# Output projection of the second block: part of its products moved between the chunks of the delta rule

## The reference, cut to what matters

```python
attn = rms_norm_2(neighbourhood_attention(aq, ak, hs(av), rpb), attn_out_g)
dn = bidirectional_gated_deltanet(dqkv, dz, dab[:, :, 0], dab[:, :, 1], ...)
x = x + jnp.concatenate([attn, dn], axis=-1) @ w_out
x = x + hierarchical_moe(rms_norm_2(x, ln2_g), ...)
```

```python
def step(state, inp):
    v_new = u_c - w_c @ state
    o_c = (q_c * exp(g_c)) @ state + qk_c @ v_new
    state = state * exp(g_last) + (k_c * exp(g_last - g_c)).T @ v_new
```

## Time and profile before

| what | value |
|---|---|
| runs | 2626.96, 2631.46, 2630.94 us; median 2630.94 us |
| the profiled execution's own time | 2627.38 us |
| its span | 2625.6 us |
| PE busy / PE weight loads busy | 2264.3 us (86%) / 1665.9 us (63%) |
| DVE / ACT / POOL busy | 1178.7 (45%) / 868.3 (33%) / 163.4 us (6%) |
| mean granted TensorE clock | 0.894 |
| moved | 377.26 MB, mean 144 GB/s |

### The profile page before, as it was taken

How to read it: one execution, slowest core, us unless ns; L and a number is a source line. 1 busy time by engine, 2 the same in 40 slices (tenths; PEclk the granted TensorE clock), 3 DMA queues, 4 the chain that set the end, 5 groups by cost and what they waited for, 6 DMA issues and landing times. The chain is left out here.

```text
span 2625.6 us, 32561 instructions
## 1 busy us (share of the span) xinstructions
PE 2264.3 (86%) x13812; PEld 1665.9 (63%) x13812; DVE 1178.7 (45%) x1868; ACT 868.3 (33%) x1294; POOL 163.4 (6%) x174
## 2 busy tenths in 40 slices
PE   8999999958997877899999899877988688888885
PEld 7787888847675775687888777656967333333332
DVE  4456664365583665575663435655343311111112
ACT  5344443255652223453442254543122110000000
POOL 0000000000001210000000000002200011111110
PEclk9899999978998777899999999967667799999998
DMA  5122222212111001222223223211014599999996
GB/s 198 65 92 85 94 99 78 99 64 100 61 65 18 14 15 49 89 83 94 96 82 100 92 89 119 79 20 17 2 49 181 239 419 416 417 409 405 403 402 253
DMA packets 106741, 377.26 MB, mean 144 GB/s; under 512 B 54976, under 2 KB 55760, under 8 KB 67680
## 3 DMA queue, kind: packets, MB, share of 16 engines
q1 hardware_dynamic: 84992, 296.44, 30.6%
q10 hardware_dynamic: 9216, 67.11, 6.2%
q0 software_dynamic: 12384, 11.58, 1.5%
HBM read 375.31 MB, written 27.53 MB: 153 GB/s over the span
## 5 line engine op out<-in xcount | busy, mean ns | idle before, releaser
L593 PE MATMUL ps<-xh,wh 128*128 128x512 f32 x1288 | 515.6, 400 | 68.5 <-DVE wl L557 45.2
L594 PE MATMUL ps<-xl,wh 128*128 128x512 f32 x1288 | 510.6, 396 | 0.0
L595 PE MATMUL ps<-xh,wl 128*128 128x512 f32 x1288 | 508.9, 395 | 0.0
L557 DVE TENSOR_TENSOR wl<-raw,wh 128x2048 fp32r<-128x2048 f32 (+2 forms) x127 | 264.3, 2081 | 285.5 <-ACT wh L551 285.5
L3462 PE MATMUL ps<-egu,XT 128*64 128x512 f32 x1088 | 273.5, 660 | 85.1 <-DMA egu<-e_up 81.3
L593 PEld LDWEIGHTS ps<-xh,wh 128*128 128x128 f32 x1288 | 247.1, 192 | 134.8 <-DVE wl L557 55.3
L595 PEld LDWEIGHTS ps<-xh,wl 128*128 128x128 f32 x1288 | 247.2, 192 | 53.7
L594 PEld LDWEIGHTS ps<-xl,wh 128*128 128x128 f32 x1288 | 247.9, 192 | 51.0 <-issue 0.2
L551 ACT ACTIVATE wh<-raw 128x2048 fp32r<-128x2048 f32 (+2 forms) x127 | 220.3, 1736 | 91.4 <-PE ps L1072 69.2
L3462 PEld LDWEIGHTS ps<-egu,XT 128*64 128x64 f32 x1088 | 94.2, 152 | 240.9 <-issue 229.4
L3480 DVE TENSOR_TENSOR HIDT<-ps,SIL 128x256 f32<-128x256 f32 x34 | 14.4, 425 | 352.0 <-ACT SIL L3472 352.0
(11 more groups left out here) (531 smaller groups left out, 3390.3 us busy)
## 6 DMA issues: line engine op xcount, KB each, us to landing
egu<-e_gate SPq DMA_DIRECT2D x68, 1024.0 KB, 14.3
egu<-e_up SPq DMA_DIRECT2D x68, 1024.0 KB, 25.3
ed<-e_down ACTq DMA_DIRECT2D x64, 1024.0 KB, 11.0
raw<-up SPq DMA_DIRECT2D x44, 1024.0 KB, 4.9
raw<-down SPq DMA_DIRECT2D x32, 704.0 KB, 4.2
raw<-rwkv_kr SPq DMA_DIRECT2D x8, 1024.0 KB, 4.9
raw<-in_dn SPq DMA_DIRECT2D x8, 1024.0 KB, 4.9
raw<-sgu_v SPq DMA_DIRECT2D x4, 1024.0 KB, 10.3
```

Of the source, the lines that this page charges most:

```text
L557: e.tensor_tensor(K.WL[s][:, 0:n], K.RAW[r][:, 0:n], K.WH[s][:, 0:n].bitcast(F32), SUB).then_inc(*K.w_low.mark(i))
L593: e.matmul(o, h[:, q, k], x_high[:, k], start=k == 0, stop=False)
L594: e.matmul(o, h[:, q, k], x_low[:, k], start=False, stop=False)
L595: last = e.matmul(o, l[:, q, k], x_high[:, k], start=False, stop=k == KT - 1)
```

## The change

- Tiles 0 to 3 of the input (the attention's features) and the first half (k = 0 to 3) of weight items 0 and 1 get buffers of their own, which overlay the attention's tiles and the old queries. SP loads these weights (2 x 512 KB) after the queries are scaled, ACT and DVE split them between the two pairs of the solve.
- PE makes four triples between w and the recurrence, then one after `s` and one after `o` in every step until twelve are done (three output tiles x four input tiles). So steps 0 to 3 have two each and steps 4 to 7 none.
- To free three PSUM banks, both directions of `ws` share bank 0, and the others move down by one.
- Item 2 and the second halves of items 0 and 1 are loaded from the end of w on, ACT splits item 2's high half after its last output copy.
- `out2_*` is written anew: fourth tile's early part, items 2 and 3, and k = 4 to 7 of the tiles begun. The squares go to a buffer of their own.
- PE's point "out2" is now taken behind the last triple.

Cut to its core (buffers, PSUM bank numbers and signals left out):

```diff
@@ delta_pe
         last.then_inc(*K.delta_sum.mark("w", x))
+    for q in range(1, 4):
+        for t in K.board.emptied(K.u["dn_w"] + q):
+            e.wait_ge(*t)
+    early = early_pe(K, e)
+    for _ in range(4):
+        next(early)
     K.board.point("PE", "solved")
...
             last.then_inc(*K.delta_sum.mark("s", s, d))
+        next(early, None)
...
         last.then_inc(*K.delta_sum.mark("o", s))
+        next(early, None)
+    for _ in early:
+        pass
@@ delta_act
         K.board.empty(u, K.act_delta("k", n))
+    for k in range(3):
+        e.activation(K.XHE[:, k], K.AT[:, k], ACT.Copy).then_inc(*K.x_high.mark("out2", k))
...
+        if pair == 0:
+            for i in range(2):
+                e.wait_ge(*K.early_in("raw", 1))
+                e.activation(K.WHE[:, i], K.RWE[:, i], ACT.Copy).then_inc(*K.w_high.mark("early", i))
+    e.activation(K.XHE3[:, :], K.AT[:, 3], ACT.Copy).then_inc(*K.x_high.mark("out2", 3))
...
+    third = K.first["out2"] + 2
+    e.wait_ge(*K.raw_in[0](third))
+    e.activation(K.WH[1][:, :], K.RAW[0][:, :], ACT.Copy).then_inc(*K.w_high.mark(third))
     K.board.point("ACT", "delta")
@@ delta_dve
+    for k in range(3):
+        x_low_dve(K, e, "out2", k, K.AT[:, k], K.XHE, K.XLE)
...
+        if pair == 0:
+            for i in range(2):
+                e.wait_ge(*K.w_high("early", i))
+                e.tensor_tensor(K.WLE[:, i], K.RWE[:, i], K.WHE[:, i].bitcast(F32), SUB).then_inc(*K.w_low.mark("early", i))
+    e.wait_ge(*K.x_high("out2", 3))
+    e.tensor_tensor(K.XLE[:, 3], K.AT[:, 3], K.XHE3[:, :].bitcast(F32), SUB).then_inc(*K.x_low.mark("out2", 3))
@@
+def early_pe(K, e, tiles=range(3)):
+
+    for i in range(2):
+        h, l = (x[:, i].rearrange("p (m k j) -> p m k j", m=2, k=4) for x in (K.WHE, K.WLE))
+        e.wait_ge(*K.w_low("early", i))
+        for k in range(4):
+            e.wait_ge(*K.x_low("out2", k))
+            for q in range(2):
+                if 2 * i + q in tiles:
+                    out2_triple(K, e, h[:, q, k], l[:, q, k], k, 2 * i + q)
+                    yield
@@ out2_sp
-    for t in K.board.all_at("delta"):
+    first, src = K.first["out2"], K.A["out2"]
+    for t in (K.delta_sum("k", 3), K.dve_delta("q", 1, 3)):
         e.wait_ge(*t)
-    load_weights(K, e, K.first["out2"], len(K.items))
+    for i in range(2):
+        e.dma_start(K.RWE[:, i].rearrange("p (m k) -> p m k", m=2), src[i].rearrange("p (m k) -> p m k", m=2)[:, :, 0:512]).then_inc(
+            *K.early_in.landing("raw", i))
+    e.wait_ge(*K.delta_sum("w", 3))
+    e.dma_start(K.RAW[0][:, :], src[2]).then_inc(*K.raw_in[0].landing(first + 2))
...
+    for i in range(2):
+        e.wait_ge(*K.w_low("half", i))
+    e.dma_start(K.RAW[1][:, :], src[3]).then_inc(*K.raw_in[1].landing(first + 3))
@@ out2_pe
+    for t in K.board.emptied(K.u["out2"] + 3 - 8):
+        e.wait_ge(*t)
+    for _ in early_pe(K, e, (3,)):
+        pass
+    whole(2, 1, range(4))
+    for i in range(2):
+        e.wait_ge(*K.w_low("half", i))
+        for k in range(4, KT):
+            e.wait_ge(*K.x_low("out2", k))
+            for q in range(2):
+                out2_triple(K, e, half_of(K.WH[0], i)[:, q, k - 4], half_of(K.WL[0], i)[:, q, k - 4], k, 2 * i + q)
+    whole(2, 1, range(4, KT))
+    whole(3, 0, range(KT))
     K.board.point("PE", "out2")
-    gemm_pe(K, e, "out2", "out2", KT, K.XH, K.XL)
@@ out2_act
-    for k in range(4):
-        e.activation(K.XH[:, k], K.AT[:, k], ACT.Copy).then_inc(*K.x_high.mark("out2", k))
-    weight_high(K, e, K.first["out2"])
+    half_high(K, e, 0)
...
+    half_high(K, e, 1)
     for h in range(4):
-        x_high_act(K, e, "out2", 4 + h, K.T[h], K.dve_delta("gated", h), K.XH)
+        x_high_act(K, e, "out2", 4 + h, K.SQO[:, h], K.dve_delta("gated", h), K.XH)
@@ out2_dve
-    for k in range(4):
-        x_low_dve(K, e, "out2", k, K.AT[:, k], K.XH, K.XL)
-    weight_low(K, e, K.first["out2"])
+    whole_low(2, 1)
+    half_low(K, e, 0)
...
         x_low_dve(K, e, "out2", 4 + h, x, K.XH, K.XL)
+        if h == 1:
+            half_low(K, e, 1)
```

More of the change, by code:

```diff
@@ L484, in uses @@
         at = 0
-        for name, n in (("sq_oo", 4), ("out2", 8), ("n_ln2", 1), ("route", 1), ("tok", 16), ("rank", 1), ("place", 1)):
+        for name, n in (("sq_oo", 5), ("out2", 8), ("n_ln2", 1), ("route", 1), ("tok", 16), ("rank", 1), ("place", 1)):
             self.u2[name] = 3000 + at
@@ L2902, in delta_pe @@
             for d, (ch, n, hf, p) in enumerate(geo):
-                last = e.matmul(K.ps[p, d, 128 * h:128 * h + 128], K.WT[:, hf, 16 * d + 4 * n + h], K.SS2[:, 0, 4 * d + h], start=True, stop=True)
+                last = e.matmul(K.ps[p, 0, 128 * h:128 * h + 128], K.WT[:, hf, 16 * d + 4 * n + h], K.SS2[:, 0, 4 * d + h], start=True, stop=True)
         last.then_inc(*K.delta_sum.mark("ws", s))
@@ L2915, in delta_pe @@
             for d, (ch, n, hf, p) in enumerate(geo):
-                last = e.matmul(K.ps[:, 2 + d, 128 * h:128 * h + 128], K.KD[p, 16 * d + 4 * n + h], K.VN[p, d, h], start=True, stop=True)
+                last = e.matmul(K.ps[:, 1 + d, 128 * h:128 * h + 128], K.KD[p, 16 * d + 4 * n + h], K.VN[p, d, h], start=True, stop=True)
         last.then_inc(*K.delta_sum.mark("kv", s))
@@ L3070, in delta_pool, with out2_rows, out2_triple @@
     K.board.point("POOL", "delta")
+def out2_rows(K, k):
+    if k < 4:
+        return K.XHE3[:, :] if k == 3 else K.XHE[:, k], K.XLE[:, k]
+    return K.XH[:, k], K.XL[:, k]
+def out2_triple(K, e, high, low, k, m):
+    o = K.ps[:, (K.u["out2"] + m) % 8]
+    xh, xl = out2_rows(K, k)
+    e.matmul(o, high, xh, start=k == 0, stop=False)
+    e.matmul(o, high, xl, start=False, stop=False)
+    last = e.matmul(o, low, xh, start=False, stop=k == KT - 1)
+    if k == KT - 1:
+        last.then_inc(*K.gemm_sum.mark("out2", m))
@@ L3082, in out2_pe, with half_low @@
+def half_low(K, e, i):
+    c = slice(1024 * i, 1024 * i + 1024)
+    e.wait_ge(*K.w_high("half", i))
+    e.tensor_tensor(K.WL[0][:, c], K.RAW[1][:, c], K.WH[0][:, c].bitcast(F32), SUB).then_inc(*K.w_low.mark("half", i))
 def out2_pe(K, e):
+    first = K.first["out2"]
     for t in K.board.all_at("delta"):
```

63 lines of the change are left out of this document (48 added, 15 removed).

## The result

| what | before | after |
|---|---|---|
| median of the runs made side by side (six each) | 2627.99 us | 2607.87 us |
| lowest and highest | 2621.87, 2631.46 us | 2604.31, 2611.99 us |
| the profiled execution: own time / span | 2627.38 / 2625.6 us | 2609.15 / 2607.0 us |
| PE busy | 2264.3 us | 2239.8 us |
| mean granted clock | 0.894 | 0.903 |

The changed kernel takes 0.9927 of the time of the one before (95% interval 0.9910 to 0.9943): it is faster, by 20.1 us, which is under 1%. The time lies in the predicted range (2580 to 2618 us), but the forecast itself, 2598 us, expected 31 us and not 20.

What follows compares the result with a forecast made beforehand. The recurrence was taken as bound by PE at half speed, on a plain chain from solve to routing. Terms -30.0 - 14.7 + 13.6 = -31.1 us on 2627.4 gave 2596.3, stated as 2598 us; range 2580 to 2618.

Steps and rivals of the forecast that it cites:

- Full clock in the recurrence: Filling PE's gap behind w keeps the recurrence at full clock, ending at 1910.9 instead of 1940.9: -30.0 us.
- The rivals of a clock that stays or falls: Recurrence at half clock throughout, 2638 to 2641 us, chance 0.14; or falling in steps 4 to 7, 2614 to 2618, 0.14.
- The steps' size: Recurrence at full clock: 6.1 us for steps 0 to 3, then 5.9 us, last step 6.1; 48.0 us in all.
- Work beside the solve: Copies on ACT, subtractions on DVE and 1 MB of loads fit idle time beside the solve: zero in sum.
- The projection: From the meeting point t0 to the last matmul 45.5 us, where it was 60.2: -14.7 us.
- The router's weights: Behind the projection, router loads queue behind ten expert loads, arriving at E+27.4 and delaying the logits: +13.6 us.
- rival 2: In the recurrence the clock holds with triples, falls in steps 4 to 7: +18.2, 2614 to 2618 us; chance 0.14.

Runs made afterwards that it cites:

- the first and third run: First: kernel before plus three unread 512-column products between w and the recurrence, 2596.9 us median; third: changed kernel with all twelve early triples there, 2606.22 us.
- the spaced kernel: The combined kernel with its two early weight loads issued at later places in the solve: 2588.62 us median, 0.9854; with early subtractions, 2580.15 us.
- the combined kernel: Changed kernel with router loads ahead of expert loads, subtractions behind the copies of u, one triple in each of eight steps: 2586.81 us median, 0.9850.

## Why the prediction was right, and where it was off

**Full clock in the recurrence: right**, and so was the reason: the change attacks the descent, and the same kernel with the gap idle lost the clock. That the clock would hold in steps 4 to 7 without triples, for which I had only the solve's row, is what the first and third run show by themselves. The rivals of a clock that stays or falls had been given 0.28.

**The steps' size: off by 3.0 us.** The term said 6.1 and 5.9 us and 48.0 in all; measured 6.53, 6.17 and 51.0. I had halved the distances of the earlier trace rows and taken 0.68 us for a triple from a long row of triples. Between products of another shape a triple takes 0.88 to 0.89 us, and the groups at full clock are more than half their old length (`ws` 1.03 for 0.95, `kv` 0.99 for 0.94, `o` 0.94 for 0.87). PE's part of a step with triples is thus 6.53 and not 5.9, and passes DVE's chain, which I had made the bound. In steps 4 to 7 `kv` comes after 2.95 us and not 2.75, `o` after 3.95 and not 3.7, and DVE's addition moves with them.

**Work beside the solve: not zero but 4.0 us.** This is the step that failed. The prediction was right about the copies and subtractions: the early ones cost about 0.2 us in the spaced kernel, and the fourth tile's nothing, since from the first product of u to that of w it is 7.1 us before and after. It dismissed the load because the DMA engines stood at 0.04. It did not ask what small transfer the load would get in the way of: PE's own program. The late 16 KB stopped PE for 1.53 us and started the next group 1.8 us late, and the stretch at 0.50 behind it added 0.58 and 0.97 us, from start to start, in the two groups that fell into it (those of 1837.16 and 1838.69). These make 3.3 of the 4.0 us. The other 0.7 lies ahead of the solve, where the clock came up to 1.00 later (5.9 us behind v, not 4.5), in the same code and ahead of the load; the runs don't tie it to the change. Nor is the stretch at 0.50 sure to follow the stop: with the same stop and all triples in the gap it did not, and v to w was 42.1 us. So what the load costs by itself is 0.8 to 1.8 us in the kernels whose clock stayed up through the solve, and 4.0 is what this one execution had.

**The projection: right, -14.2 for -14.7 predicted.** ACT's exponentials end at 1930.5, 10.5 us behind the meeting point (predicted 10.3), and k = 7 is split at 22 us, as worked out; the rest is a short stretch at half clock, 1939.8 to 1943.2.

**The router's weights: right, +15.0 for +13.6.** The bias landed 22.8 us after its issue at E+5.9, so at E+28.7. I had the bytes' time (24.3 us) and 2 us of start; with the router's own bytes these make E+27.0, and not the E+27.4 written there. The Trainium skill ("DMA: Bandwidth & Descriptors", section "Queues, rings and completion order") lets a completion come only after the earlier writes of the same DMA engine. This case's 22.8 us for the bias behind ten loads, against 2.7 when it was issued ahead of them, agree with that; a queue that moves its loads in the order of their issue would look the same.

**The clock and a busy PE.** The Trainium skill ("TensorE: Matmul & The Clock Gate", section "What's actually happening") says that activity releases the throttle. If activity meant a busy engine, the windows of the recurrence would speak against it: busy 92% at 0.50 before, busy 82% at 1.00 with the gap filled.

In all: gap and recurrence -26.9 for -30.0, solve +4.0 for 0, projection -14.2 for -14.7, router +15.0 for +13.6. Together -22.1 for -31.1; a further 3.5 us between the profiled executions lie ahead of v and behind the logits, which the change doesn't touch. All four misses have the same sign, so nothing cancelled; 2607.87 us lies in the range only because the range had been drawn wide for rival 2, which did not happen.

## What to carry to other kernels

Ask of a short idle time of PE what the clock does behind it: here one of 2.5 us had cost some 30 us in a stretch that did not climb back, and three throwaway products cured it. When a point at which "buffers are free" moves, look at what stands behind the released loads on the queue, and let small transfers that something waits for go first. And a load into idle DMA engines isn't free if an engine's own program comes through them: a wait that ends in "issue" is to be compared with the instruction queue's transfers before any engine beside it is blamed.

## What the hardware showed that I had not expected

- Once down, the clock stays down in a busy recurrence: 0.50 from 1861.4 to 1946.7, with PE busy 92% from 1861 to 1941, while triples of 512 columns between the same products brought it back within one step.
- The same stop didn't always bring the clock down. 1.53 us in the solve did in the changed kernel; 1.54 us at the same product, with all triples in the gap, did not:

```profile
1837.40:1840.80 3.40, 3.40 (x72) 3.40 (x69) 0.10 (x1) 1.81 (x3) 0.00 (x0) 0.50 0.00 0
```

```profile
1833.00:1837.00 4.00, 3.53 (x121) 3.43 (x119) 1.49 (x3) 2.80 (x4) 0.00 (x0) 1.00 0.02 4
```

  Likewise the combined kernel had half clock from 1931.0 to 1937.8 and took 48.1 us for the projection, the one with spaced loads had 1.00 throughout and took 45.8, with the same waits of PE ahead of it (2.25 us at 1930.2 in both). What decides between them stays open; it moves a kernel's time by 2 us.
- The same subtraction took 1.33 us beside GpSimd's products and 0.74 us later (2.22 for three), and GpSimd's eight products 9.40 us beside the subtractions and 8.03 without: the two slowed each other. The timelines of GpSimd in the changed and in the combined kernel:

```profile
1824.30 9.40 POOL L3088 TENSOR_TENSOR KG<-KKT,dBG 128x512 f32<-128x512 f32 x8
```

```profile
1820.38 8.03 POOL L3087 TENSOR_TENSOR KG<-KKT,dBG 128x512 f32<-128x512 f32 x8
```
